# Fifteen gate units of two gated feed-forward layers computed with seven half-size products instead of eight, with part of the extra work on GpSimd

## The chip, the cores and the metric

The kernel runs on one NeuronCore of a Trainium2 chip. The metric is the time of one execution on the device in microseconds. The median of 3 runs before the change is 1631.95 us.

## The reference

Two transformer blocks act one after the other on 512 rows of width 1024, all in float32. The change touches only the gated feed-forward of the second block, which comes twice (l = 0 and 1; below "layer 0" and "layer 1"):

```python
def conv_ffn(h, w_gate, w_val, conv_w, conv_b, w_out):
    a = h @ w_gate                                   # 512x1024 @ 1024x2816
    ap = jnp.pad(a, ((0, 0), (CONV_W - 1, 0), (0, 0)))
    a = ap[:, 0:S] * conv_w[0] + ap[:, 1:S + 1] * conv_w[1] + ap[:, 2:S + 2] * conv_w[2] + conv_b
    return (jax.nn.silu(a) * (h @ w_val)) @ w_out
```

Ahead of it stands an RMS norm of h. The first block has an ungated MLP (4096 wide, squared ReLU), in which 11 of 16 "up" units are already computed in the way that the change brings to the gates.

## The kernel before

**Units.** All weights come from HBM as units of up to 128x2048 floats (1 MB), in a fixed list, PLAN. A unit of a gate or value matrix holds 256 output features for all 1024 inputs, so 11 gate units and 11 value units make a layer (`gate0 0` to `gate0 10`, `val0 0` and so on), and `fo0 0` to `fo0 11` are the units of the output matrix. Gate and value units alternate; the four output units of a group of pairs come after the first pair of the next group: gate 0, val 0, ..., gate 4, val 4, fo 0 to 3, gate 5, ..., val 8, fo 4 to 7, gate 9, ..., val 10, fo 8 to 11.

**Precision.** Each float32 operand is split into a high part (rounded to the type that TensorE takes) and a low part (what is left). ScalarE makes the high part of a unit (WH from RAW, line 1493), VectorE the low part (WL, line 1914); both together are called a split here. A product is then three matmuls: high by high, high by low, low by high (lines 728 to 730). The activations' parts are AH and AL, 8 tiles of 128x512. A normal unit is 2 output tiles of 8 x 3 matmuls with 512 columns, so 48 matmuls.

**Buffers.** RAW has two units, WH and WL have three, and each is used in turn. So a unit can be split while the two units before it are in TensorE. PSUM has 8 banks; FFN tiles take 7 of them in turn (`next_bank(7)`), and a bank is free again when VectorE has read it.

**Work behind a tile.** A gate tile m: VectorE multiplies PSUM by the norm's factors rb (line 2571) and does the three taps of the convolution (2573, 2575, 2577), ScalarE does SiLU (1833). A value tile m: VectorE multiplies by rb (2581) and by the gate (2583), ScalarE makes the high part HH (1838), VectorE the low part HL (2585), and ten such tiles (NH) are kept for the output units.

**Order.** Every engine walks the same generator (`ffn_order`) and does its own share of each step, waiting on counting semaphores. The order on an engine is thus the order in the code: in the turn of unit u first the split of unit u + 2, then the two tiles of u and what follows them. An engine never passes a waiting instruction. SyncE loads the units in order, each as soon as RAW is free.

**The fast form.** For the "up" units in FAST the weight unit is held as 2x2 blocks of 512 columns and the activations as 2x2 blocks of 256 rows (Winograd's form of Strassen's scheme). Seven products of half size, called a, c, g, d, e, b, f in the order in which TensorE does them, each of 4 x 3 matmuls with 256 columns, take the place of eight: 84 matmuls of 256 columns. It takes seven weight blocks (four raw or summed in place, three sums in `stage`; `added` makes the sums) and as many activation blocks (TH and TL, made by `shapes`), and the results are put together with extra additions (`mid`, `turned`, `row1`, `row2`). The seven blocks lie in a ring of 12 places, WHR and WLR, which is the same memory as WH and WL; a normal unit takes four.

Of the kernel before, what the change touches and what calls it, by code (L numbers as in the profile page):

```python
# [133 lines left out]
def low_is_in(k, m):  # L134

    return (k.POOL if UNIT["up", m // 2] in FAST else k.DVE)("hl", "down", m)

# [108 lines left out]
def memory(nc, ctx):  # L246
# [106 lines left out]
    a.at = inner  # L353
    k.cvs = [a.tile(f"cvs{i}", [P, S]) for i in range(2)]
# [88 lines left out]
def turn_order(u):  # L443
# [21 lines left out]
    if u + 1 in FAST:  # L465
        yield "part", u + 1, "stageA"
    if after and fast:
        yield "post", m
    if fast:
        yield "mid", u  # L470
        yield "turned", u
    if after and fast:
        yield "low", m
    if u + 1 in FAST:
        yield "part", u + 1, "stageB"
    if fast:
        yield "row2", u
        yield "post", 2 * i + 1
# [34 lines left out]

def ffn_order(l):

    pairs = ffn_pairs()
    for g in range(4):
        if g < 3:
            yield from pair_order(l, pairs[g][0])
        if g > 0:  # L520
            for i in range(4):
                yield "split", UNIT[f"fo{l}", 4 * (g - 1) + i] + 2
                yield "down", g - 1, 2 * i
                yield "down", g - 1, 2 * i + 1
        for j in pairs[g][1:] if g < 3 else ():
            yield from pair_order(l, j)
# [183 lines left out]
def tensor_program(k, e):  # L710
# [426 lines left out]
    def down(name, g, n, base, kc, m):  # L1137
# [36 lines left out]
    def form_product(u, x, bs):  # L1174
# [16 lines left out]
    def fast_products(u):  # L1191

        m = 2 * PLAN[u][1]
        bs = range(4) if PLAN[u][1] % 2 else range(4, 8)
# [3 lines left out]
        form_product(u, "a", bs)  # L1198
        w.wait_ge(WLO("stageB", u))
        form_product(u, "c", bs)  # L1200
        w.wait_ge(*free[bs[2]])
        form_product(u, "g", bs)
        form_product(u, "d", bs)
        w.wait_ge(*free[bs[3]])
        form_product(u, "e", bs)
        w.wait_ge(*free[bs[1]])
        form_product(u, "b", bs)
        form_product(u, "f", bs)
        for name in (("up", m), ("up", m + 1), ("unit", u)):
            MM.also(*name)  # L1210
        free[bs[0]], free[bs[1]], free[bs[2]], free[bs[3]] = [DVE("y", u)], [DVE("row", m)], [DVE("row", m + 1)], [DVE("z", u)]

    for step, *x in mlp_order():
# [31 lines left out]
        elif step == "mid":  # L1245
            fast_products(*x)
# [70 lines left out]
    def ffn(l, norm, n0, added):  # L1317
        for step, *x in ffn_order(l):
# [31 lines left out]
            elif step == "tile":  # L1350
                y, m = x
                u = UNIT[f"{('gate', 'val')[y]}{l}", m // 2]
                b = next_bank(7)
# [127 lines left out]
def scalar_program(k, e):  # L1481
    w = Waits(e)
    bank, cst, par, X, AH, sq, t2s = k.bank, k.cst, k.par, k.X, k.AH, k.sq, k.t2s
    MM, ACT, DVE, POOL, WHI = k.MM, k.ACT, k.DVE, k.POOL, k.WHI
# [217 lines left out]

    def free_high(name, m, n0, group_of):
# [19 lines left out]
    for step, *x in mlp_order():  # L1723
# [18 lines left out]
        elif step == "part":  # L1742
            u, part = x
            w.wait_ge(loaded(k, u), DVE("s2" if part[:5] == "stage" else "s4", u),
                      *(MM(*name) for name in held_until(u, *PARTS[part])))
            for h, _, cols in ring_views(k, u, *PARTS[part]):
                t = e.activation(h, part_source(k, u, part)[:, cols], AF.Copy)  # L1747
            t.then_inc(*WHI.mark(part, u))
        elif step == "mid":
            u, = x  # L1750
            before = max((v for v in FAST if v < u), default=0)
# [67 lines left out]

    def ffn(l, norm, n0, seen):  # L1820
        name = f"fo{l}"
        group_of = lambda m: min(m // 8, 2)
        for step, *x in ffn_order(l):
# [77 lines left out]
def vector_program(k, e):  # L1901
# [497 lines left out]

    def added(u):  # L2400

        raw = k.RAW[RAW_OF[u]][:, :].rearrange("p (c n) -> p c n", c=4)
        before = max((v for v in FAST if v < u), default=0)
# [29 lines left out]
    for step, *x in mlp_order():  # L2433
# [14 lines left out]
        elif step == "part":  # L2448
            u, part = x
            w.wait_ge(WHI(part, u))  # L2450
            for h, l, cols in ring_views(k, u, *PARTS[part]):
                t = e.tensor_tensor(l, part_source(k, u, part)[:, cols], h.bitcast(F), SUB)  # L2452
            t.then_inc(*WLO.mark(part, u))
            if part == "rawB":
                WLO.also(u)
# [95 lines left out]

    def ffn(l, norm, n0):
        name = f"fo{l}"
        for step, *x in ffn_order(l):
# [6 lines left out]
            elif step == "rest":  # L2561
                y, m = x
                i, s = m % 2, m % NH
                a, t, v = k.t1s[i], t2s[i], k.cvs[i]
                w.wait_ge(MM("ffn", l, y, m), ACT("rb", norm))
                if y == 0:
                    tap = [par[:, PC_CW + 66 * l + 22 * j + m:PC_CW + 66 * l + 22 * j + m + 1] for j in range(3)]
                    w.wait_ge(POOL("zeroed", l))
                    if m > 1:
                        w.wait_ge(DVE("conv", l, m - 2), DVE("gated", l, m - 2))  # L2570
                    e.tensor_tensor(a[:, 2:], bank[where["ffn", l, 0, m]][:, :], rb[:, :], MUL).then_inc(*DVE.mark("ffn", l, 0, m))
                    w.wait_ge(DVE("ffn", l, 0, m))
                    e.tensor_scalar(t[:, :], a[:, 0:S], tap[0], None, MUL).then_inc(*DVE.mark("tap0", l, m))
                    w.wait_ge(DVE("tap0", l, m))
                    e.scalar_tensor_tensor(t[:, :], a[:, 1:S + 1], tap[1], t[:, :], MUL, ADD).then_inc(*DVE.mark("tap1", l, m))
                    w.wait_ge(DVE("tap1", l, m))
                    e.scalar_tensor_tensor(t[:, :], a[:, 2:S + 2], tap[2], t[:, :], MUL, ADD).then_inc(*DVE.mark("conv", l, m))  # L2577
                else:
                    if m > 1:
                        w.wait_ge(DVE("hl", name, m - 2))  # L2580
                    e.tensor_tensor(v[:, :], bank[where["ffn", l, 1, m]][:, :], rb[:, :], MUL).then_inc(*DVE.mark("ffn", l, 1, m))
                    w.wait_ge(DVE("ffn", l, 1, m), ACT("silu", l, m))
                    e.tensor_tensor(v[:, :], v[:, :], t[:, :], MUL).then_inc(*DVE.mark("gated", l, m))  # L2583
                    w.wait_ge(ACT("hh", name, m))
                    e.tensor_tensor(k.HL[s][:, :], v[:, :], k.HH[s][:, :].bitcast(F), SUB).then_inc(*DVE.mark("hl", name, m))
# [89 lines left out]
def pool_program(k, e):  # L2675
# [17 lines left out]

    w.wait_ge((k.x_in[7], 16))
# [54 lines left out]
    root(4)  # L2749
# [19 lines left out]
    root(6)  # L2769
# [202 lines left out]
```

## Time and profile before

| | us |
|---|---|
| median of 3 runs (1630.81 to 1632.61) | 1631.95 |
| the profiled execution | 1633.97 |
| its span | 1632.2 |
| TensorE busy | 1625.4 |
| VectorE busy | 1015.7 |
| ScalarE busy | 660.1 |
| GpSimd busy | 115.0 |

The profile is of one execution. "Busy" of an engine is the time in which it had an instruction running; "span" is from the first to the last instruction. Layer 0 of the feed-forward runs from about 656 to 1018 us, layer 1 from about 1268 us to the end. Matmuls are pipelined, so the distance between two starts, not the duration of one, is what a matmul costs.

### The profile page before, as it was taken

How to read it: one execution, taken by the hardware profiler on the slowest of the kernel's cores; microseconds unless marked ns; L12 is line 12 of the kernel's file. 1: busy time of each engine (PE TensorE's matmuls, PEld its weight loads, DVE VectorE, ACT ScalarE, POOL GpSimd, SP SyncE). 2: the span in 40 equal slices, each digit the busy share in tenths (PEclk: the TensorE clock that was granted, in tenths of full speed). 3: DMA queues.
4: the chain of work that ended last, by engine and by line, in shares of the span. 5: the costliest groups of instructions: out<-in, count | busy, mean ns of one | idle time of the engine just before them, and what ended most of it. 6: DMA issues, size and time to landing. Idle time of an engine off the chain costs nothing.

```text
span 1632.2 us, 20194 instructions
## 1 busy us (share of the span) xinstructions
PE 1625.4 (100%) x8480; PEld 1347.1 (83%) x8480; DVE 1015.7 (62%) x1523; ACT 660.1 (40%) x919; POOL 115.0 (7%) x102
## 2 busy tenths in 40 slices
PE   9999999999999999999999999999999999999999
PEld 7877878898989888888888888877777888888887
DVE  6797664696756757577466357546655576366353
ACT  5576435344444446433222223456565333122221
POOL 1300000011111100000000000312101100000000
PEclk9999999999999999999999999999999999999999
DMA  5310228355464521223222213322221223222311
GB/s 188 112 41 27 104 78 120 82 111 138 86 138 85 162 78 64 80 102 116 104 103 90 111 64 123 102 87 94 76 77 52 78 103 108 100 102 97 110 59 71
DMA packets 28059, 156.01 MB, mean 96 GB/s; under 512 B 3712, under 2 KB 5392, under 8 KB 12096
## 3 DMA queue, kind: packets, MB, share of 16 engines
q1 hardware_dynamic: 26352, 149.75, 25.8%
q0 software_dynamic: 1328, 4.86, 5.3%
q8 instruction: 67, 1.10, 0.3%
q14 instruction: 24, 0.20, 0.0%
q10 hardware_dynamic: 288, 0.10, 0.0%
HBM read 149.98 MB, written 4.72 MB: 95 GB/s over the span
## 4 chain that ended last, share of the span: by engine, by line
PE 75%; DVE 2%; ACT 1%; issue 1%; POOL 0%; DVEq 0%; ACTq 0%
PE bank L728 20%; PE bank L729 19%; PE bank L730 19%; PE bank L734 3%; PE bank L736 2%; PE bank L735 2%; PE bank L1186 2%; PE bank L1188 2%; PE bank L1187 2%; PE bank L1424 1%; PE bank L1434 1%; PE bank L1450 1%; DVE WLR L2452 1%; PE bank L1310 0%; ACT WHR L1747 0%
## 5 line engine op out<-in xcount | busy, mean ns | idle before, releaser
L1914 DVE TENSOR_TENSOR WL<-RAW,WH 128x2048 fp32r<-128x2048 f32 (+2 forms) x122 | 273.0, 2243 | 193.5 <-ACT WH L1493 193.5
L728 PE MATMUL bank<-AH,WH 128*128 128x512 f32 (+1 forms) x974 | 382.9, 393 | 0.4 <-DVE WL L1964 0.3
L730 PE MATMUL bank<-AH,WL 128*128 128x512 f32 (+1 forms) x974 | 379.2, 389 | 0.0
L729 PE MATMUL bank<-AL,WH 128*128 128x512 f32 (+1 forms) x974 | 379.2, 389 | 0.0
L1493 ACT ACTIVATE WH<-RAW 128x2048 fp32r<-128x2048 f32 (+2 forms) x122 | 227.0, 1867 | 171.9 <-PE bank L730 138.0
L728 PE MATMUL bank<-HH,WH 128*128 128x512 f32 x608 | 236.6, 389 | 0.0
L729 PE MATMUL bank<-HL,WH 128*128 128x512 f32 x608 | 236.5, 389 | 0.0
L730 PE MATMUL bank<-HH,WL 128*128 128x512 f32 x608 | 236.5, 389 | 0.0
L728 PEld LDWEIGHTS bank<-AH,WH 128*128 128x128 f32 (+1 forms) x974 | 182.5, 187 | 41.9 <-issue 2.4
L730 PEld LDWEIGHTS bank<-AH,WL 128*128 128x128 f32 (+1 forms) x974 | 182.5, 187 | 38.8
L729 PEld LDWEIGHTS bank<-AL,WH 128*128 128x128 f32 (+1 forms) x974 | 182.5, 187 | 38.3 <-issue 1.0
L730 PEld LDWEIGHTS bank<-HH,WL 128*128 128x128 f32 x608 | 114.1, 188 | 23.8
L728 PEld LDWEIGHTS bank<-HH,WH 128*128 128x128 f32 x608 | 114.1, 188 | 23.7
L729 PEld LDWEIGHTS bank<-HL,WH 128*128 128x128 f32 x608 | 114.1, 188 | 23.4
L1944 DVE TENSOR_TENSOR X<-X,bank 128x512 f32<-128x512 f32 x79 | 54.0, 685 | 117.5 <-PE bank L730 117.5
L1833 ACT ACTIVATE t2s<-t2s,par 128x512 f32<-128x512 f32 x44 | 31.9, 724 | 186.6 <-DVE t2s L2577 186.6
L734 PE MATMUL bank<-WH,AH 128*128 128x512 f32 x224 | 89.9, 401 | 0.0
L736 PE MATMUL bank<-WH,AL 128*128 128x512 f32 x224 | 87.5, 391 | 0.0
L735 PE MATMUL bank<-WL,AH 128*128 128x512 f32 x224 | 87.3, 390 | 0.0
L1838 ACT ACTIVATE HH<-cvs 128x512 fp32r<-128x512 f32 x44 | 27.8, 633 | 126.0 <-DVE cvs L2583 126.0
L1500 ACT ACTIVATE sq<-X 128x512 f32<-128x512 f32 x49 | 30.9, 630 | 59.4 <-DVE X L1944 55.3
L734 PEld LDWEIGHTS bank<-WH,AH 128*128 128x128 f32 x224 | 42.0, 188 | 10.8 <-issue 2.3
(347 smaller groups left out, 2379.3 us busy)
## 6 DMA issues: line engine op xcount, KB each, us to landing
RAW<-in_W SPq DMA_DIRECT2D x124, 1024.0 KB, 4.8
RAW<-in_W SPq DMA_DIRECT2D x9, 768.0 KB, 4.2
X<-in_XT SPq DMA_DIRECT2D x16, 256.0 KB, 5.5
ev_scratch<-ev POOLq DMA_DIRECT2D x16, 160.0 KB, 7.6
Gb<-ev_scratch SPq DMA_DIRECT2D x16, 128.0 KB, 3.1
Gb<-ev_scratch SPq DMA_DIRECT2D x16, 112.0 KB, 2.7
out<-X SPq DMA_DIRECT2D x7, 256.0 KB, 2.0
RAW<-in_W SPq DMA_DIRECT2D x2, 512.0 KB, 6.0
```

Source lines behind the costliest of these rows:

```text
L728: e.matmul(o, a, h, start=first, stop=False)
L729: e.matmul(o, a, l, start=False, stop=False)
L730: return e.matmul(o, c, h, start=False, stop=last)
L734: e.matmul(o, h, a, start=first, stop=False)
L735: e.matmul(o, h, c, start=False, stop=False)
L736: return e.matmul(o, l, a, start=False, stop=last)
L1186: e.matmul(o, a, h, start=c == 0 and x in "ageb", stop=False, skip_group_check=True)
L1187: e.matmul(o, a, lo, start=False, stop=False, skip_group_check=True)
L1188: t = e.matmul(o, l, h, start=False, stop=c == 3, skip_group_check=True)
L1493: e.activation(k.WH[SLOT_OF[u]][:, 0:n], k.RAW[RAW_OF[u]][:, 0:n], AF.Copy).then_inc(*WHI.mark(u))
L1914: e.tensor_tensor(k.WL[j][:, 0:n], k.RAW[RAW_OF[u]][:, 0:n], k.WH[j][:, 0:n].bitcast(F), SUB).then_inc(*WLO.mark(u))
L1944: e.tensor_tensor(X[:, m, :], X[:, m, :], src, ADD).then_inc(*DVE.mark("x", n, m))
```

## The change

Fifteen gate units join FAST: `gate0 4` to `gate0 10` and `gate1 3` to `gate1 10`. The order of the units stays. What comes with it:

- the activations' blocks FH and FL (four forms of 256 columns for each of 4 chunks c), made once a layer, in the turns of three early units (FORMS_IN): GpSimd adds high and low parts ("sum", two instructions of 128x512), VectorE makes four forms ("form", four of 128x256), ScalarE makes their high parts (two of 128x512), GpSimd their low parts ("formed", two of 128x512);
- the weight sums of a fast gate are made on GpSimd (one instruction of 128x1024 and two of 128x512, step "add"), in the turn of the unit two before it; its seven blocks are split in four parts ("part": 1024, 1024, 1024 and 512 columns) on ScalarE and VectorE in the turn of the unit just before it;
- the low parts HL of value tiles go from VectorE to GpSimd;
- the first tap of the fast tiles goes to ScalarE;
- the value tile's own buffer (cvs) is gone: the gate's tile t2s is multiplied by rb and then by the value's PSUM tile, so a value tile's bank is free only after that second multiplication (`DVE.also("ffn", l, 1, m)`);
- steps "mid", "turned", "row1", "row2" and "conv" put a fast gate's tiles together.

```diff
+FIRST_GATE = (4, 3)
 FAST = {UNIT["up", i] for i in range(FIRST_FAST, 16)}
+FAST |= {UNIT[f"gate{l}", j] for l in range(2) for j in range(FIRST_GATE[l], 11)}
...
+FORMS_IN = ({("gate", 2): (0, 1), ("val", 2): (2,), ("gate", 3): (3,)},
+            {("gate", 1): (0, 1), ("val", 1): (2,), ("gate", 2): (3,)})
 def ffn_order(l):
+    first = 2 if l == 0 else 1
+    for j in range(first):
+        yield from pair_order(l, j)
+    for u in range(UNIT[f"gate{l}", first], UNIT[f"fo{l}", 11] + 1):
+        yield from ffn_turn(l, u)
+def ffn_turn(l, u):
+    for c in forms:
+        yield "sum", c
+    if behind:
+        yield "row1", u - 1
+    if u + 1 in FAST:
+        for part in PARTS:
+            yield "part", u + 1, part
+    for v in (u + 1, u + 2):
+        if v < len(PLAN) and v not in FAST and turn_of(v) == u:
+            yield "split", v
+    for c in forms:
+        yield "form", c
+        yield "formed", c
+    if u + 2 in FAST:
+        yield "add", u + 2
+    if fast:
+        yield "mid", u
+        yield "turned", u
+        yield "row2", u
+    elif name == "fo":
+        yield "down", i // 4, 2 * (i % 4)
+        yield "down", i // 4, 2 * (i % 4) + 1
+    else:
+        if behind:
+            yield "conv", i
+        for m in (2 * i, 2 * i + 1):
+            yield "tile", int(name == "val"), m
+            yield "rest", int(name == "val"), m
...
+    def set_of(u):
+        return range(4) if PLAN[u][1] % 2 else range(4, 8)
+    def fast_gate(l, u):
+        w.wait_ge(*(POOL("formed", l, c) for c in range(4)))
+        bs = fast_products(u, k.FH, k.FL, "dceg")
...
+            elif step == "form":
+                w.wait_ge(POOL("sum", l, c))
+                if c > 0:
+                    w.wait_ge(POOL("formed", l, c - 1))
...
+            elif step == "sum":
+                if c > 0:
+                    w.wait_ge(DVE("f4", l, c - 1))
+                for i, z in enumerate((k.stage[:, 2, :], k.fx[c][:, :])):
+                    t = e.tensor_tensor(z, k.AH[:, 4 * i + c, :].bitcast(F), k.AL[:, 4 * i + c, :].bitcast(F), ADD)
+                t.then_inc(*POOL.mark("sum", l, c))
+            elif step == "formed":
+                for n in range(2):
+                    w.wait_ge(ACT("fh", l, c, n), DVE("f4", l, c))
+                    t = e.tensor_tensor(k.FL[:, c, 2 * n:2 * n + 2, :], k.stage[:, n, :].rearrange("p (i n) -> p i n", i=2),
+                                        k.FH[:, c, 2 * n:2 * n + 2, :].bitcast(F), SUB)
+                t.then_inc(*POOL.mark("formed", l, c))
```

How the change moves instructions at three places. First, VectorE in layer 0 before the change, from the end of gate unit 2 to the beginning of value unit 3 (WL is a unit's low part, cvs and HL belong to a value tile, t1s and t2s to a gate tile):

```order
L1914 TENSOR_TENSOR WL_59<-RAW_54,WH_56 128x2048
L2581 TENSOR_TENSOR cvs_169<-bank,rb 128x512
L2583 TENSOR_TENSOR cvs_169<-cvs_169,t2s_69 128x512
L2585 TENSOR_TENSOR HL_140<-cvs_169,HH_130 128x512
...
L1914 TENSOR_TENSOR WL_60<-RAW_55,WH_57 128x2048
L2571 TENSOR_TENSOR t1s_146<-bank,rb 128x512
...
L1914 TENSOR_TENSOR WL_61<-RAW_54,WH_58 128x2048
L2581 TENSOR_TENSOR cvs_169<-bank,rb 128x512
```

The same place after the change (WLR is the ring of low parts; the four WLR instructions are the parts of `gate0 4`, the first fast gate):

```order
L2676 TENSOR_TENSOR t1s_147<-bank,rb 128x512
L2678 TENSOR_SCALAR t2s_70<-t1s_147,par 128x512
L2656 SCALAR_TENSOR_TENSOR t2s_70<-t1s_147,par,t2s_70 128x512
L2658 SCALAR_TENSOR_TENSOR t2s_70<-t1s_147,par,t2s_70 128x512
L2497 TENSOR_TENSOR WLR<-RAW_55,WHR 128x1024 x2
L2497 TENSOR_TENSOR WLR<-stage,WHR 128x1024
L2497 TENSOR_TENSOR WLR<-stage,WHR 128x512
L2682 TENSOR_TENSOR t2s_69<-t2s_69,rb 128x512
L2684 TENSOR_TENSOR t2s_69<-t2s_69,bank 128x512
```

Before, the weights of gate unit 4 were split ahead of the two tiles of gate unit 3; now its parts stand behind them, one unit before TensorE wants them, and only the two value tiles of unit 3 follow.

Second, GpSimd in layer 0 after the change, from the low parts of value tiles 2 and 3 to the sums of the first fast gate. Before, GpSimd had nothing here at all.

```order
L2848 TENSOR_TENSOR HL3_139<-t2s1_70,HH3_129 128x512
L2857 TENSOR_TENSOR stage_65<-AH_52,AL_53 128x512
L2857 TENSOR_TENSOR fx0_171<-AH_52,AL_53 128x512
...
L2863 TENSOR_TENSOR FL_170<-stage_65,FH_169 128x512 x4
...
L2848 TENSOR_TENSOR HL5_141<-t2s1_70,HH5_131 128x512
L2857 TENSOR_TENSOR stage_65<-AH_52,AL_53 128x512
L2857 TENSOR_TENSOR fx3_174<-AH_52,AL_53 128x512
L2863 TENSOR_TENSOR FL_170<-stage_65,FH_169 128x512 x2
L2871 TENSOR_TENSOR stage_65<-RAW1_55 128x1024
L2874 TENSOR_TENSOR stage_65<-RAW1_55,stage_65 128x512
L2876 TENSOR_TENSOR RAW1_55<-RAW1_55,stage_65 128x512
```

All sums, forms' low parts, value tiles' low parts and weight sums stand in one queue.

Third, VectorE in layer 1 after the change, around the parts of `gate1 3`, the first fast gate there (with the bank numbers):

```order
L2497 TENSOR_TENSOR WLR_63<-RAW1_55,WHR_62 128x1024 x2
L2497 TENSOR_TENSOR WLR_63<-stage_65,WHR_62 128x1024
L2497 TENSOR_TENSOR WLR_63<-stage_65,WHR_62 128x512
L2682 TENSOR_TENSOR t2s0_69<-t2s0_69,rb_64 128x512
L2684 TENSOR_TENSOR t2s0_69<-t2s0_69,bank6 128x512
L2682 TENSOR_TENSOR t2s1_70<-t2s1_70,rb_64 128x512
L2684 TENSOR_TENSOR t2s1_70<-t2s1_70,bank0 128x512
```

and TensorE's first matmul of that unit:

```order
L1226 MATMUL bank0<-AH_52,WHR_62 128x256
```

The last of the four instructions on value tiles reads bank 0, into which the first product of the fast gate writes.

## Rows read from the trace of the kernel before

**Rows 1.** The page's first part: busy time of each engine.

```profile
PE 1625.4 (100%) x8480; PEld 1347.1 (83%) x8480; DVE 1015.7 (62%) x1523; ACT 660.1 (40%) x919; POOL 115.0 (7%) x102
```

**Rows 2.** TensorE's waits: for whom, us in total, times, longest.

```profile
PE bank L1186 <- DVE WLR L2452: 0.8, 2, 0.4
```

**Rows 3.** TensorE's timeline, at three borders between units of the feed-forwards.

```profile
810.81 0.39 PE L728 MATMUL bank<-AH,WH 128*128 128x512 f32 x1
...
897.85 0.39 PE L728 MATMUL bank<-HH,WH 128*128 128x512 f32 x1
...
1378.76 0.39 PE L728 MATMUL bank<-HH,WH 128*128 128x512 f32 x1
```

**Rows 4.** TensorE's timeline, four fast up units: starts of products a, g, d, e.

```profile
423.86 0.28 PE L1186 MATMUL bank<-AH,WHR 128*128 128x256 f32 x1
...
426.67 0.28 PE L1186 MATMUL bank<-AH,WHR 128*128 128x256 f32 x1
...
428.09 0.29 PE L1186 MATMUL bank<-TH,WHR 128*128 128x256 f32 x1
...
429.47 0.28 PE L1186 MATMUL bank<-TH,WHR 128*128 128x256 f32 x1
...
463.21 0.40 PE L728 MATMUL bank<-HH,WH 128*128 128x512 f32 x1
```

**Rows 5.** VectorE's timeline, layer 0, in brackets the idle time before and its releaser.

```profile
698.10 0.68 DVE L2581 TENSOR_TENSOR cvs<-bank,rb 128x512 f32<-128x512 f32 x1
...
704.74 2.29 DVE L1914 TENSOR_TENSOR WL<-RAW,WH 128x2048 fp32r<-128x2048 f32 x1 [1.11 <-ACT WH L1493]
...
721.18 0.69 DVE L2571 TENSOR_TENSOR t1s<-bank,rb 128x512 f32<-128x512 f32 x1
...
723.88 0.69 DVE L2571 TENSOR_TENSOR t1s<-bank,rb 128x512 f32<-128x512 f32 x1
...
729.26 2.29 DVE L1914 TENSOR_TENSOR WL<-RAW,WH 128x2048 fp32r<-128x2048 f32 x1 [2.60 <-ACT WH L1493]
731.47 0.68 DVE L2581 TENSOR_TENSOR cvs<-bank,rb 128x512 f32<-128x512 f32 x1
732.19 0.69 DVE L2583 TENSOR_TENSOR cvs<-cvs,t2s 128x512 f32<-128x512 f32 x1
...
745.05 0.75 DVE L2577 SCALAR_TENSOR_TENSOR t2s<-t1s,par,t2s 128x512 f32<-128x512 f32 x1
```

**Rows 6.** ScalarE's timeline, layer 0: SiLU of gate tile 5 and the split behind it.

```profile
726.70 0.72 ACT L1833 ACTIVATE t2s<-t2s,par 128x512 f32<-128x512 f32 x1 [1.97 <-DVE t2s L2577]
727.33 1.90 ACT L1493 ACTIVATE WH<-RAW 128x2048 fp32r<-128x2048 f32 x1
```

**Rows 7.** GpSimd's timeline in the MLP: low parts of up tiles.

```profile
364.29 1.67 POOL L2734 TENSOR_TENSOR HL<-t2s,HH 128x512 fp32r<-128x512 f32 x1 [3.24 <-ACT HH L1721]
...
384.73 1.30 POOL L2734 TENSOR_TENSOR HL<-t2s,HH 128x512 fp32r<-128x512 f32 x1 [0.56 <-ACT HH L1721]
```

**Rows 8.** Groups by shape in the MLP (330 to 545 us): busy us, mean ns.

```profile
L2452 DVE TENSOR_TENSOR WLR<-RAW,WHR 128x1024 fp32r<-128x1024 f32 x20 | 23.7, 1222 | 6.7 <-ACT WHR L1747 6.7
...
L2459 DVE TENSOR_TENSOR YZ<-G,bank 128x256 f32<-128x256 f32 x11 | 4.6, 418 | 2.6 <-ACT G L1753 2.6
...
L1747 ACT ACTIVATE WHR<-RAW 128x1024 fp32r<-128x1024 f32 x20 | 20.2, 1053 | 51.2 <-DVE RAW L2410 34.1 <-PE bank L730 9.4 <-issue 7.7
```

**Rows 9.** VectorE's timeline, layer 1: the first gate tile.

```profile
1293.29 0.69 DVE L2571 TENSOR_TENSOR t1s<-bank,rb 128x512 f32<-128x512 f32 x1
```

**Rows 10.** TensorE in one stretch: busy us (instructions), granted clock, DMA share, GB/s.

```profile
192.00:198.40 6.40, 6.40 (x18) 0.50 0.00 0
```

**Rows 11.** TensorE's timeline ahead of and in the stretch of rows 10.

```profile
190.58 2.33 PE L1075 MATMUL bank<-cst,sq 128*128 128x1 f32 x16
...
194.20 0.63 PE L728 MATMUL bank<-OM,WH 128*128 128x512 f32 x1
194.63 0.63 PE L729 MATMUL bank<-LM,WH 128*128 128x512 f32 x1
```

More of the change, by code:

```diff
@@ L352, in memory @@
               enumerate([base + 4 * S * 8] + [base + 4 * S * (NH + 8) + 4 * 4 * BW * i for i in range(3)])]
-    a.at = inner
-    k.cvs = [a.tile(f"cvs{i}", [P, S]) for i in range(2)]
+    a.at = inner + 192
+    k.FH = a.tile("FH", [P, 4, 4, 256], R)
+    fl_at = a.at
+    k.FL = a.tile("FL", [P, 4, 4, 256], R)
+    k.fx = [a.over(f"fx{c}", [P, S], fl_at + 4 * 1024 * c) for c in range(4)]
     a.at = base
@@ L466, in turn_order @@
         yield "part", u + 1, "stageA"
+        yield "part", u + 1, "stageB"
     if after and fast:
         yield "post", m
+        yield "low", m
     if fast:
@@ L471, in turn_order @@
         yield "turned", u
[L472 to L476, printed above, removed]
         yield "row2", u
@@ L511, in up_order @@
             yield "rest", m
+FORMS_IN = ({("gate", 2): (0, 1), ("val", 2): (2,), ("gate", 3): (3,)},
+            {("gate", 1): (0, 1), ("val", 1): (2,), ("gate", 2): (3,)})
 def ffn_order(l):
[L516 to L526, printed above, removed]
+    first = 2 if l == 0 else 1
[4 more added lines that the diff above has]
+def ffn_turn(l, u):
+    name, i = PLAN[u][0][:-1], PLAN[u][1]
+    fast, behind = u in FAST, u - 1 in FAST
+    forms = FORMS_IN[l].get((name, i), ())
+    for c in forms:
[26 more added lines that the diff above has]
+            yield "rest", int(name == "val"), m
 def pair_order(l, j):
@@ L1699, in scalar_program, with part_high @@
     split(UNIT["up", 0] + 1)
+    def part_high(u, part, adder):
+        w.wait_ge(loaded(k, u))
+        if part != "rawA":
+            w.wait_ge(adder("s2" if part[:5] == "stage" else "s4", u))
+        w.wait_ge(*(MM(*name) for name in held_until(u, *PARTS[part])))
+        for h, _, cols in ring_views(k, u, *PARTS[part]):
+            t = e.activation(h, part_source(k, u, part)[:, cols], AF.Copy)
+        t.then_inc(*WHI.mark(part, u))
     def free_high(name, m, n0, group_of):
@@ L1743, in scalar_program @@
             u, part = x
[L1744 to L1748, printed above, removed]
+            part_high(u, part, DVE)
         elif step == "mid":
             u, = x
-            before = max((v for v in FAST if v < u), default=0)
+            before = fast_before(u)
             w.wait_ge(MM("form", u, "c"), DVE("row", 2 * PLAN[before][1]) if before else DVE("t4", 3))
@@ L2448, in vector_program @@
         elif step == "part":
[L2449 to L2455, printed above, removed]
+            part_low(*x)
         elif step == "mid":
@@ L2768, in pool_program @@
     t.then_inc(*POOL.mark("zeroed", 1))
-    root(6)
+    ffn(1, 6)
 def sync_program(k, e):
```

209 lines of the change are left out of this document (160 added, 49 removed).

## The prediction

> **What bounds the kernel now.** I read the page's busy shares first: TensorE is busy 1625.4 of 1632.2 us, VectorE 62% [rows 1]. Then TensorE's waits: the longest kind in the whole program is 0.8 us in two waits, on the weights of fast up units, and none falls into the feed-forwards [rows 2]. So the time is TensorE's issue time, and a change gains what it takes from that and loses every wait that it makes. Third, TensorE's timeline: eight units from 810.81 to 897.85 take 87.04 us, 10.88 each, with nothing between [rows 3].
>
> The lower shares of the others do not mean that they keep up. Value tile 0 of layer 0 was begun by VectorE at 698.10, and gate unit 3's last tap ends at 745.8 [rows 5]. Counting back six units from 810.81, gate unit 4 starts in TensorE at 745.53, value unit 3 at 734.65 [rows 3]. VectorE thus stands a unit behind TensorE after each norm. Today that costs nothing, since weights are split two units ahead.
>
> **What the change removes.** Four fast up units take 39.35 us, 9.84 each; a product that reads AH takes 1.42 (426.67 to 428.09), one that reads TH 1.38 [rows 4]. In the new gates product g reads the made forms too, and most of the others follow a made one, so I take 9.77. A unit saves 1.11 us, fifteen 16.6. Bounds: 9.84 gives 15.6; FH no faster than AH, at some 0.12 per matmul (84 x 0.12 = 10.08), gives 12.0.
>
> **What it adds, steady state.** Per pair VectorE gains 1536 split columns and the five combinations, and loses two HL and two first taps. Worked from one gate's start: split of the value unit done at +6.4, combinations by +8.3, first row at +10.6 behind product f, the four parts by +15, taps by +20.3, last value tile by +22.3, that is 1.6 us into the next gate, as it began. TensorE wants the value weights at +9.8 and the next gate's at +20.6, so it has 3.4 and more to spare: 0 us. GpSimd has some 8 us per 20.6. If that cover went, each pair would lose what is missing. Only at the last value unit is the new route of HL (high part on ScalarE, 0.63 to the next as between 726.70 and 727.33, then GpSimd 1.3) [rows 6, 7] a little late for the sixth chunk of `fo 8`: 0.3 us a layer.
>
> **What it adds at the start of each layer.** This decides. The row prices: gate tile 2.70 (721.18 to 723.88), two-instruction value tile 1.42 (pitch 0.72 and 0.70), a split in VectorE 2.21, a split that begins behind the last tap's SiLU 2.66 later (726.6 to 729.26) [rows 5, 6]; GpSimd 1.30 per 512 columns with two inputs, where 1.67 occurs [rows 7]; a part of 1024 columns 1.05 on ScalarE and 1.22 on VectorE, 256 columns 0.42 [rows 8], so four forms 1.7 (estimate). For 1024 columns on GpSimd I take 2 x 1.30.
>
> Layer 0 from 698.10, in program order. VectorE: value tiles 0 and 1 to 700.9; split of val 2 (behind ScalarE's) 703.4 to 705.65; gate tiles 2 and 3 to 711.05; value tiles to 713.9; split of gate 3 to 718.6. GpSimd's low parts end at 715.9, its first sum at 718.5. Form 0 to 720.3. Now form 1 needs sum 1 and "formed 0", four GpSimd instructions behind form 0: 725.5; form 1 to 727.3. Gate tiles 4 and 5 to 732.7. The split of val 3 is queued behind their SiLU: 735.3 to 737.5, and TensorE wants it at 734.65: **2.9 us**. Form 2 to 739.2, value tiles to 742.05. Form 3 needs sum 3, which stands behind formed 2 and two low parts, six instructions: 747.1; form 3 to 748.8. Gate tiles 6 and 7 to 754.2. Only now the parts of gate 4: ScalarE's first 754.9, VectorE's 756.0 to 757.2. TensorE ended val 3 at 748.4: **8.8 us**. GpSimd's weight sums (formed 3, then 5.2) end at 756.7, so rawB is done at 759.0 and stageB, for which product c waits, at 760.9. Product a ends at 758.6: **2.3 us**. Layer 0: 14.0.
>
> Layer 1 from 1293.29 [rows 9], one unit earlier in everything; gate 3 would start at 1378.76 - 4 x 10.88 = 1335.2 [rows 3]. The same walk: split of val 2 at 1325.15 against 1324.36, **0.8**; form 1 waits to 1313.2, form 3 to 1334.8; gate tiles to 1341.9; rawA at 1344.85, stageB at 1348.55. Here the first product also writes bank 0, which held value tile 5, and that bank is free only after its second multiplication, four instructions (2.8) behind the parts: 1351.4. TensorE is free at 1336.1: **15.3 us**, and c waits no more. Layer 1: 16.1. Without the bank it would be 8.8 + 2.3 as above, 4.2 less.
>
> Behind this VectorE is level with TensorE, and the later fast gates start without a wait.
>
> **TensorE's clock.** From 192.0 to 198.4 us the granted clock is 0.50, the lower level of 1.2 GHz, and 512-column matmuls stand 0.43 apart, not 0.227; just before, the engine did 16 matmuls of one column in 2.33 us [rows 10, 11]. An idle of 9 or 15 us should lower it too. Lost there: 6.4 x (1 - 0.227/0.43) = 3.0 us. Part of it falls into the wait for c in layer 0, so I take 1.5 + 3.0 = **4.5 us**, bounds 0 and 6.
>
> The Trainium skill, "TensorE: Matmul & The Clock Gate", section "HAM oscillation — how this bites in real kernels", says that gaps in which TensorE idles throttle it again and the work behind them runs at the lower clock. Its idle case is not in this trace; by the row alone, which has only light work, the 4.5 might be 0, and the sum 1646.
>
> **Sum.** -16.6 + 14.0 + 16.1 + 0.6 + 4.5 = +18.6. The profiled execution, 1633.97, becomes 1652.6; the median of the runs, 1631.95, lies 2 us below and becomes 1650.6, 1.1% slower. GpSimd at 1.67 instead of 1.30 on the ten instructions that form 1 and form 3 wait for costs 3.7 a layer, +7.4; FH at AH's pace +4.6; no clock loss -4.5; no bank wait -4.2.
>
> **Rivals.**
> *Faster: the start costs less than the gain.* Place: the first fast gates; mechanism: VectorE is not held by GpSimd, so sums and low parts run ahead. With the two waits per layer (5.2 and 5.0) and the bank wait gone, VectorE reaches the parts some 10 us earlier, about 744, and each layer loses 3 to 4: -16.6 + 7 = 1622. It decides in favour when a layer's start costs under 8.3 us. For it: GpSimd is idle here today [rows 1]. Against: each form waits for instructions that cannot be issued earlier, and the order is fixed. Chance 0.11.
> *GpSimd is slower than its rows.* The 128x1024 sums with a broadcast operand, and all sums beside VectorE, cost 1.67 per 512 or more. Starts +7.4, and if a low part then comes too late in each pair, 1 us on each of 15: 1660 to 1672. For it: rows of 1.67 while VectorE works; against: most rows are 1.30, and VectorE mostly waits there. Chance 0.17.
> The skill, "GPSIMD Engine Reference", section "Elementwise — side-by-side cycle accounting", holds that a two-input operation takes GpSimd about twice VectorE's time because both inputs share one read port. By that rule this work should stay where it was; 1.30 against 0.69 agrees.
> *The early stalls are there but TensorE gains nothing else*, the half-size products at 0.12: inside the range. *The change does nothing to the time* (gain and starts cancel at 8.3 a layer): 0.04.
>
> **How the numbers follow.** Forecast 0.68, slower by GpSimd 0.17, faster 0.11, same 0.04. Three runs tell 0.2% from nothing. The range leaves out the faster case and most of the second: low, no clock loss, no bank wait and 3 us of luck in waits, 1639; high, half of GpSimd's surcharge and FH's pace, 1660.
>
> **What would show it.** Right: a new wait of TensorE on VectorE's WLR of about 9 us near 748 and one of about 15 near 1336 on a value tile's second multiplication; two VectorE waits on GpSimd of about 5 us ahead of each; granted clock 0.5 behind both; units at 9.8 with no wait from the second fast gate on. Wrong: the parts of the first fast gate done before TensorE is free; or waits in every pair, on WL (VectorE too late) or on the sums (GpSimd too slow).

## The result and the profile after

The changed kernel takes 1664.27 us (median of 4 runs, 1664.17 to 1665.38) against 1632.28 of before (4 runs, 1630.81 to 1633.17): ratio 1.0201, 95% interval 1.0188 to 1.0213. It is 32 us slower where 18.6 were forecast: the sign is right, the time lies above the range. The profiled execution has a span of 1662.5 us, 30.3 more than before.

The page's first part; columns as in [rows 1]:

```profile
PE 1615.6 (97%) x9020; PEld 1363.0 (82%) x9020; DVE 1076.5 (65%) x1601; ACT 720.3 (43%) x1025; POOL 313.0 (19%) x223
```

TensorE now does less (1615.6 us busy, 1625.4 before) and is no longer always busy. GpSimd's busy time has gone from 115.0 to 313.0. The second view is the list of TensorE's waits (for whom, us in total, times, longest), which answers to [rows 2]:

```profile
PE bank L1226 <- DVE t2s L2684: 16.5, 1, 16.5
PE bank L768 <- DVE WL L2007: 12.8, 2, 7.3
PE bank L1226 <- DVE WLR L2497: 12.3, 1, 12.3
```

These four waits are 41.6 us, all ahead of or at the first fast gate of a layer, and no later unit waits. TensorE's timeline gives their places: value unit 3 and gate unit 4 of layer 0, value unit 2 and gate unit 3 of layer 1, with the matmul that follows each of the two gates, and one later fast gate for comparison:

```profile
737.63 0.79 PE L768 MATMUL bank<-AH,WH 128*128 128x512 f32 x1 [7.28 <-DVE WL L2007]
...
762.48 0.55 PE L1226 MATMUL bank<-AH,WHR 128*128 128x256 f32 x1 [12.26 <-DVE WLR L2497]
...
774.92 0.40 PE L768 MATMUL bank<-AH,WH 128*128 128x512 f32 x1
...
829.35 0.28 PE L1226 MATMUL bank<-AH,WHR 128*128 128x256 f32 x1
...
839.10 0.40 PE L768 MATMUL bank<-AH,WH 128*128 128x512 f32 x1
...
850.01 0.28 PE L1226 MATMUL bank<-AH,WHR 128*128 128x256 f32 x1
...
1342.27 0.80 PE L768 MATMUL bank<-AH,WH 128*128 128x512 f32 x1 [5.50 <-DVE WL L2007]
...
1372.69 0.55 PE L1226 MATMUL bank<-AH,WHR 128*128 128x256 f32 x1 [16.46 <-DVE t2s L2684]
...
1383.83 0.40 PE L768 MATMUL bank<-AH,WH 128*128 128x512 f32 x1
```

A later fast gate takes 839.10 - 829.35 = 9.75 us, and with the value unit behind it, to 850.01, 20.66 where the pair took 2 x 10.88 before: 1.10 less, so the gain is as forecast (1.11). The first ones take 12.44 (762.48 to 774.92) and 11.14 (1372.69 to 1383.83). The value units ahead of them take 12.59 (737.63 to 750.22, where the next wait begins) and 13.96 (1342.27 to 1356.23) instead of 10.88. The granted clock behind each wait says why (TensorE in a stretch, as in [rows 10], with the other engines between):

```profile
737.70:740.70 3.00, 3.00 (x7) 2.41 (x8) 2.86 (x7) 1.38 (x3) 1.38 (x1) 0.50 0.74 216
741.00:750.00 9.00, 9.00 (x41) 7.32 (x39) 3.42 (x8) 1.89 (x4) 7.13 (x6) 1.00 0.08 32
762.50:768.00 5.50, 5.50 (x25) 5.43 (x26) 5.18 (x7) 1.59 (x4) 0.76 (x1) 0.50 0.57 194
768.00:775.00 7.00, 7.00 (x62) 7.00 (x62) 4.07 (x5) 2.63 (x3) 1.82 (x2) 1.00 0.15 39
1342.30:1348.00 5.70, 5.70 (x14) 4.44 (x15) 4.24 (x8) 2.41 (x4) 4.04 (x3) 0.50 0.50 184
1372.70:1375.60 2.90, 2.90 (x13) 2.90 (x14) 0.56 (x1) 2.31 (x2) 2.77 (x3) 0.50 0.02 6
```

The first, third, fifth and sixth stretch, one behind each of the four waits, are at 0.50, the lower level of 1.2 GHz; together the four units behind waits are 2.7 + 1.4 + 1.7 + 3.1 = 8.9 us too long.

So the span splits into -16.6 (gain), +41.6 (waits), +8.9 (clock), and -4.5, because VectorE's first gate tile of layer 0 comes that much earlier than before (688.24 against 692.70). Some 2.9 of this is the half-clock stretch of [rows 10], which this execution does not have. The rest are the first four fast up units, which take 39.35 where they took 40.91; 0.8 of that are the two waits of [rows 2], and the change, which also reorders some steps of the fast up units, has neither. The sum is +29.4 of the 30.3.

Now VectorE's timeline in layer 0, gate tile 6 and the start of tile 7, the last work ahead of the first fast gate's parts; in the prediction such a tile costs 2.70:

```profile
749.02 0.69 DVE L2676 TENSOR_TENSOR t1s<-bank,rb 128x512 f32<-128x512 f32 x1
749.75 1.23 DVE L2678 TENSOR_SCALAR t2s<-t1s,par 128x512 f32<-128x512 f32 x1
751.01 1.65 DVE L2656 SCALAR_TENSOR_TENSOR t2s<-t1s,par,t2s 128x512 f32<-128x512 f32 x1
752.69 2.71 DVE L2658 SCALAR_TENSOR_TENSOR t2s<-t1s,par,t2s 128x512 f32<-128x512 f32 x1
755.33 0.68 DVE L2676 TENSOR_TENSOR t1s<-bank,rb 128x512 f32<-128x512 f32 x1
```

And GpSimd's in the same layer, first behind the low parts of value tiles 2 and 3, then beside the rows above:

```profile
712.60 3.37 POOL L2857 TENSOR_TENSOR fx<-AH,AL 128x512 f32<-128x512 f32 x1
717.64 1.29 POOL L2857 TENSOR_TENSOR stage<-AH,AL 128x512 f32<-128x512 f32 x1 [1.67 <-DVE stage L2699]
...
752.25 2.60 POOL L2871 TENSOR_TENSOR stage<-RAW 128x1024 f32<-128x1024 f32 x1
```

The tap that begins at 752.69 takes 2.71, and the GpSimd sum that is under way ends at 754.85. GpSimd's own sum at 712.60 takes 3.37: VectorE's split was running then (711.86, for 2.94) and ended at 714.80. The one at 717.64, beside an idle VectorE, takes 1.29. Rows that read a bank keep their 0.68. Summed over VectorE's operations from 688 to 762 us, 8.6 us are above their durations in the kernel before, and 8.9 in the same part of layer 1 (1305 to 1373 us); VectorE's waits for GpSimd, 5.27 and 5.41, are as forecast (5.2 and 5.0). That is the theory to be tested: **contention**, VectorE's operations whose tensors are all in SBUF stretched by GpSimd's. The rival is **waits only**: VectorE's standing for GpSimd costs the time, and the long rows have another cause.

### The profile page after: what moved, and what is told of

It is laid out like the page before. It is cut to its first block, busy times and chain, and to the rows that moved or that the text cites. A ratio compares the mean times of both kernels' runs of the same rounds, so it can differ in the third digit from the quotient of the medians.

```text
span 1662.5 us, 21669 instructions
## 1 busy us (share of the span) xinstructions
PE 1615.6 (97%) x9020; PEld 1363.0 (82%) x9020; DVE 1076.5 (65%) x1601; ACT 720.3 (43%) x1025; POOL 313.0 (19%) x223
## 4 chain that ended last, share of the span: by engine, by line
PE 88%; DVE 6%; POOL 3%; ACT 2%; issue 1%; DMA 0%; SPq 0%; DVEq 0%
PE bank L768 18%; PE bank L769 18%; PE bank L770 18%; PE bank L1226 5%; PE bank L1228 5%; PE bank L1227 5%; PE bank L774 3%; PE bank L776 3%; PE bank L775 3%; PE bank L1484 1%; PE bank L1023 1%; PE bank L1494 1%; PE bank L1510 1%; DVE t2s L2656 1%; DVE t2s L2658 1%; PE bank L1008 1%
## 5 line engine op out<-in xcount | busy, mean ns | idle before, releaser
L768 PE MATMUL bank<-AH,WH 128*128 128x512 f32 (+1 forms) x734 | 291.8, 398 | 13.2 <-DVE WL L2007 12.8
L769 PE MATMUL bank<-AL,WH 128*128 128x512 f32 (+1 forms) x734 | 287.6, 392 | 0.0
L770 PE MATMUL bank<-AH,WL 128*128 128x512 f32 (+1 forms) x734 | 287.3, 391 | 0.0
L768 PEld LDWEIGHTS bank<-AH,WH 128*128 128x128 f32 (+1 forms) x734 | 138.5, 189 | 45.7 <-DVE WL L2007 13.6
L770 PEld LDWEIGHTS bank<-AH,WL 128*128 128x128 f32 (+1 forms) x734 | 138.4, 189 | 29.9
L1226 PE MATMUL bank<-AH,WHR 128*128 128x256 f32 x356 | 101.7, 286 | 28.7 <-DVE t2s L2684 16.5
L2848 POOL TENSOR_TENSOR HL<-t2s,HH 128x512 fp32r<-128x512 f32 x44 | 56.9, 1294 | 318.1 <-ACT HH L1908 316.2
L1770 ACT ACTIVATE WHR<-RAW 128x1024 fp32r<-128x1024 f32 (+1 forms) x54 | 53.8, 1022 | 138.8 <-PE bank L770 75.9
L1228 PE MATMUL bank<-AH,WLR 128*128 128x256 f32 x356 | 101.6, 285 | 0.0
L1227 PE MATMUL bank<-AL,WHR 128*128 128x256 f32 x356 | 101.4, 285 | 0.0
L1226 PEld LDWEIGHTS bank<-AH,WHR 128*128 128x128 f32 x356 | 68.8, 193 | 30.1 <-issue 29.5
```

The lines of the kernel that those rows point to most:

```text
L768: e.matmul(o, a, h, start=first, stop=False)
L769: e.matmul(o, a, l, start=False, stop=False)
L770: return e.matmul(o, c, h, start=False, stop=last)
L1226: e.matmul(o, a, h, start=c == 0 and x in "ageb", stop=False, skip_group_check=True)
L1227: e.matmul(o, a, lo, start=False, stop=False, skip_group_check=True)
L1228: t = e.matmul(o, l, h, start=False, stop=c == 3, skip_group_check=True)
```

## The experiments

Each line tells the edit against the changed kernel, unless it says otherwise. Beside the runs stands the kernel before on the same chip: 1631.78 (runs 1 to 4), 1632.26 (5 to 8) and 1631.81 (9).

**1. No fast gates, no forms.**

```
FIRST_GATE = (11, 11)
FORMS_IN = ({}, {})
```

> Control: the changed kernel with no fast gate and no form; what is left of the change are the low parts of value tiles on GpSimd, values in the gate's tile and the banks. In the trace of the changed kernel the excess over before is 41.6 us of waits at the first fast gates, some 9 us of clock behind them, 16.6 us of gain, and a start of layer 0 that is 4.4 us earlier. If that account is right, without gates and forms the time is that of before, 1632, within 2 us (low parts of the sixth chunk late by 0.3 a layer, clock period at 192 us there or not). If instead GpSimd's low parts slow VectorE in every pair so much that TensorE waits, it is 1636 or more.

One wait that named the last part of a fast gate names the plain unit's weights here.

Measured: 1629.18 us (10 runs), ratio 0.9989 (0.9979 to 0.9998); no wait of TensorE in the feed-forwards. Values in the gate's tile, their low parts on GpSimd and the banks cost nothing. That it is 2.6 us less than before fits the two differences ahead of layer 0 named above: no half-clock stretch in the profiled execution, and 39.35 us for the first four fast up units. The 0.6 us for the sixth chunk of `fo 8` is not there. All that is lost comes with the forms and the fast gates.

**2. Forms in the fo turns, first fast gate at gate 5.**

```
FIRST_GATE = (5, 5)
FORMS_IN = ({("fo", 0): (0, 1), ("fo", 1): (2,), ("fo", 2): (3,)},) * 2
```

> Forms in the turns of fo 0 to 2 and the first fast gate at gate 5 in both layers: 12 fast gates instead of 15. All theories that put the loss at the start of a layer, where VectorE stands a unit behind, say that the waits go: gain 12 x 1.11 = 13.3, start costs 0, 0.6 for the sixth chunk: 1632.3 - 13.3 + 0.6 = 1619.6, within 2; no wait of TensorE above 1 us. If the contention of GpSimd and VectorE also costs where VectorE has slack, the forms in the fo turns bring waits of some us a layer and the time is 1624 to 1630. If the fast gates do not gain what the borders of units say, it is 1630 or more.

Measured: 1618.26 us (4 runs), ratio 0.9920 (0.9905 to 0.9935): faster than both kernels. TensorE waits for nothing here, while VectorE still waits for GpSimd as long as ever (for whom, total, times, longest):

```profile
DVE stage L2693 <- POOL fx L2856: 15.7, 6, 4.2
DVE stage L2693 <- POOL FL L2862: 10.5, 2, 5.3
```

These 26.2 us cost nothing: they lie where VectorE has only to add blocks to X. Against run 1 twelve gates bring 10.9 us by the medians and 12.0 between the fastest executions (1628.62 and 1616.57); by the borders of units it would be 12 x 1.10 = 13.2. Between the profiled executions it is 10.5, and some 1.7 more when the half-clock stretch, which only run 2's has (granted clock 0.83 from 190 to 200 us), is set aside; about 1 us stays unexplained.

**3. Forms and the first weight sums on VectorE, in their old places.**

```
-    for c in forms:
+    for c in forms[:1]:
         yield "sum", c
...
     for c in forms:
         yield "form", c
+        if c + 1 in forms:
+            yield "sum", c + 1
         yield "formed", c
```

The steps "sum", "formed" and the first fast gate's "add" are taken from GpSimd's program into VectorE's, with the same operations.

> The forms' sums and low parts and the first fast gate's weight sums on VectorE instead of GpSimd; nothing else is moved. Work added on VectorE ahead of the first fast gate: 8 sums of 0.69, 8 low parts of 0.75, weight sums 2.6, in all 14.1 us; waits of VectorE for GpSimd that go: 1.2 + 5.3 + 5.4 = 11.9 us. Contention theory (VectorE's operations with all inputs in SBUF are stretched while GpSimd runs its two-input operations, 8.6 us in the trace of layer 0): the stretch goes too, the first product of gate0 4 stands 6 to 9 us earlier than in the changed kernel (754 to 756 instead of 762.5) and the same in layer 1: 1664.3 - 13 to 18 = 1646 to 1651; the taps of gate tiles 4 to 7 take 0.49, 0.75, 0.75. Waits-only theory (what cost is VectorE standing for GpSimd, the long taps are something else, as traffic of DMA or of ScalarE): 14.1 - 11.9 = 2.2 us later a layer, long taps stay: 1668.

Measured: 1650.96 us (4 runs), ratio 1.0122 (1.0105 to 1.0139), 13.3 less than the changed kernel. The same gate tile 6 in VectorE's timeline:

```profile
746.48 0.68 DVE L2678 TENSOR_TENSOR t1s<-bank,rb 128x512 f32<-128x512 f32 x1
747.19 0.48 DVE L2680 TENSOR_SCALAR t2s<-t1s,par 128x512 f32<-128x512 f32 x1
747.71 0.75 DVE L2658 SCALAR_TENSOR_TENSOR t2s<-t1s,par,t2s 128x512 f32<-128x512 f32 x1
748.50 0.75 DVE L2660 SCALAR_TENSOR_TENSOR t2s<-t1s,par,t2s 128x512 f32<-128x512 f32 x1
```

and the first product of gate unit 4 in TensorE's:

```profile
755.05 0.55 PE L1228 MATMUL bank<-AH,WHR 128*128 128x256 f32 x1 [11.83 <-DVE WLR L2499]
```

It begins 7.4 us earlier than in the changed kernel (762.48), although VectorE has 13.6 us more work even at undisturbed durations (16 instructions of 0.69 and 2.6 of weight sums), and every tap has its old duration. Waits only had this kernel 2.2 us a layer later; it falls. What stays is VectorE's lateness itself: TensorE still waits 11.8 and, in layer 1, 17.4 us.

**4. Value tile 5 of layer 1 in bank 4.**

```
b = ... if u - 1 in FAST else 4 if (l, y, m) == (1, 1, 5) else next_bank(7)
```

> Only the bank of value tile 5 of layer 1 is changed, from 0 to 4, so that the first product of gate1 3 does not wait for that tile's second multiplication. In the trace of the changed kernel the part that product a needs is ready at 1366.9 (first half of the pair of low parts from 1365.66), product a began at 1372.69; with stageB ready at 1369.75 product c then waits under 1 us. Expected: 5 us less, 1659.3, in the place of TensorE's 16.5 us wait one of some 11 us on the weights. The prediction had 4.2 for this step. If the bank is not what ends the wait, the time stays 1664.

Measured: 1660.99 us (4 runs), ratio 1.0181 (1.0165 to 1.0196): 3.3 less, not 5.0 (4.5 less between the profiled executions, whose layers 1 begin at the same time, 1305.54 and 1305.56). TensorE's timeline in layer 1:

```profile
1354.33 0.80 PE L768 MATMUL bank<-AH,WH 128*128 128x512 f32 x1 [4.09 <-DVE t1s L2676]
...
1367.06 0.55 PE L1226 MATMUL bank<-AH,WHR 128*128 128x256 f32 x1 [5.66 <-DVE WLR L2497]
```

The first product begins where its weights are done, at 1367.06, 5.6 earlier: the bank was what ended the wait. But bank 4 held a gate tile that the late VectorE had not read, so the value tile waited 4.1, and the gate behind the shorter waits took 11.85, 0.7 more than 11.14. My expectation had looked at one wait and not at the next.

**5. GpSimd at side work in the kernel before.** Sixteen sums of two tiles that nothing else touches, then sixteen copies; nobody waits for them.

```
+    for n in range(32):
...
+        if n < 16:
+            t = e.tensor_tensor(k.side[n % 2][:, :], k.side[2][:, :], k.side[3][:, :], ADD)
+        else:
+            t = e.tensor_copy(k.side[n % 2][:, :], k.side[2][:, :])
```

> The kernel before, with work for GpSimd that nobody reads or waits for, in the first gate tiles of layer 0: 16 sums of two tiles of 128x512, then 16 copies of one such tile. VectorE's program is unchanged, and none of its tiles is touched by GpSimd. Contention theory: beside the sums VectorE's first tap goes from 0.49 to about 1.2, the other taps from 0.75 to about 1.65, a split from 2.29 to about 2.9, while multiplications that read a bank stay at 0.69; sums take more than 1.30 there. Beside the copies the stretch is smaller or none, if it is a matter of GpSimd's second input; if it is the same, any work of GpSimd does it. Theory of other traffic: VectorE's rows stay as before. The time stays within 2 us of before, since VectorE's work has cover of about a unit.

VectorE beside the sums, from 690 to 716 us, by shape (busy us, mean ns):

```profile
L2576 DVE SCALAR_TENSOR_TENSOR t2s<-t1s,par,t2s 128x512 f32<-128x512 f32 x3 | 5.0, 1664 | 0.1
...
L2574 DVE TENSOR_SCALAR t2s<-t1s,par 128x512 f32<-128x512 f32 x3 | 3.2, 1072 | 0.1
L2572 DVE TENSOR_TENSOR t1s<-bank,rb 128x512 f32<-128x512 f32 x4 | 2.7, 680 | 0.0
L2584 DVE TENSOR_TENSOR cvs<-cvs,t2s 128x512 f32<-128x512 f32 x2 | 2.1, 1062 | 0.1
```

the same operations with GpSimd idle, from 726 to 767 us:

```profile
L2576 DVE SCALAR_TENSOR_TENSOR t2s<-t1s,par,t2s 128x512 f32<-128x512 f32 x4 | 3.0, 751 | 0.1
L2584 DVE TENSOR_TENSOR cvs<-cvs,t2s 128x512 f32<-128x512 f32 x4 | 2.8, 693 | 0.1
...
L2574 DVE TENSOR_SCALAR t2s<-t1s,par 128x512 f32<-128x512 f32 x4 | 1.9, 486 | 0.1
```

the first gate tile beside the copies, in VectorE's timeline:

```profile
767.30 0.92 DVE L2574 TENSOR_SCALAR t2s<-t1s,par 128x512 f32<-128x512 f32 x1
768.25 0.98 DVE L2576 SCALAR_TENSOR_TENSOR t2s<-t1s,par,t2s 128x512 f32<-128x512 f32 x1
```

and GpSimd's two kinds, from 690 to 800 us:

```profile
L2762 POOL TENSOR_TENSOR side<-side,side 128x512 f32<-128x512 f32 x16 | 27.3, 1743 | 11.9 <-DVE t1s L2572 11.9
L2764 POOL COPY side<-side 128x512 f32<-128x512 f32 x16 | 13.8, 909 | 49.1 <-DVE t1s L2572 49.1
```

A tap goes from 0.75 to 1.66, the first tap (one tensor input, in SBUF, 0.49) to 1.07 in the mean (0.79 to 1.62), a product of two SBUF tiles from 0.69 to 1.06; what reads a bank stays at 0.68. The one split that lies wholly beside the sums takes 2.50 where it took 2.29; 2.9 was expected. Beside copies a tap takes 0.98. In the kernel before, with GpSimd idle, the gate tile at 692.70 has its first tap at 0.48 and the others at 0.75, so it is not the place in the layer. The contention is shown, without any dependence between the engines. The rest of my expectation was wrong: the time was 1641.54 (one execution), 9 more, as VectorE was slowed so much that TensorE waited 6.4 us for gate unit 3's weights. The unit of cover that I had counted was not there so soon behind the norm.

**6. TensorE held ahead of five gates of the kernel before**, for chains of 1, 2, 4, 6 and 9 sums of GpSimd.

```
LADDER = {5: 1, 6: 2, 7: 4, 9: 6, 10: 9}
...
+    w.wait_ge(POOL("held", m // 2, LADDER[m // 2] - 1))
```

> The kernel before, in which TensorE stands still ahead of gate units 5, 6, 7, 9 and 10 of layer 0, for a chain of 1, 2, 4, 6 and 9 sums of GpSimd: about 1.3, 2.6, 5.4, 8 and 12 us. It measures the clock term alone. In the changed kernel idle times of 5.5, 7.3, 12.3 and 16.5 us were followed by granted clock 0.5 and by units that were about 3.0, 1.6, 2.7 and 1.4 us too long. If any idle time of some us costs about the same, the units behind the last three are 1.5 to 3 us too long whatever its length, and those behind 1.3 and 2.6 us show whether there is a length that costs nothing. If the price grows with the idle time, 12 us cost twice what 5.4 do. Whole time: 1632 + 29 idle + 6 to 9 clock = 1667 to 1670, and less where VectorE's lead is given back nowhere.

Measured: 1669.91 us (one execution), span 1668.1. The idle times, in TensorE's timeline:

```profile
809.01 0.50 PE L730 MATMUL bank<-AH,WH 128*128 128x512 f32 x1 [1.18 <-POOL side L2760]
833.73 0.79 PE L730 MATMUL bank<-AH,WH 128*128 128x512 f32 x1 [2.62 <-POOL side L2760]
862.36 0.80 PE L730 MATMUL bank<-AH,WH 128*128 128x512 f32 x1 [5.18 <-POOL side L2760]
960.74 0.79 PE L730 MATMUL bank<-AH,WH 128*128 128x512 f32 x1 [8.69 <-POOL side L2760]
997.61 0.80 PE L730 MATMUL bank<-AH,WH 128*128 128x512 f32 x1 [12.16 <-POOL side L2760]
```

and the clock in the stretch behind each:

```profile
809.00:816.00 7.00, 6.99 (x31) 5.75 (x32) 3.43 (x3) 0.85 (x1) 0.00 (x0) 1.00 0.35 137
833.70:844.00 10.30, 10.27 (x39) 8.40 (x40) 5.50 (x6) 1.82 (x2) 0.00 (x0) 0.86 0.29 103
862.30:873.00 10.70, 10.64 (x36) 8.63 (x37) 4.55 (x5) 0.00 (x0) 0.00 (x1) 0.76 0.28 98
960.70:971.00 10.30, 10.26 (x33) 8.20 (x34) 1.76 (x3) 0.00 (x0) 0.00 (x0) 0.72 0.00 0
997.60:1008.00 10.40, 10.39 (x40) 8.48 (x41) 2.69 (x4) 0.42 (x1) 0.00 (x0) 0.86 0.00 0
```

The wait of 1.18 us was followed by no loss of clock. Behind the others (1 - clock) x length gives 1.4, 2.6, 2.9 and 1.5 us: 12.2 us of idle time cost no more than 2.6. The span grew by 35.9, of which 29.8 are idle time; the rest, 6.1, with the 3.0 of [rows 10] that this execution lacks, is near the sum 8.4. So each of the four longer waits cost one to three us of clock, and the changed kernel has four waits of such length.

**7. Fast gates in layer 0 alone.**

```
FIRST_GATE = (4, 11)
FORMS_IN = ({("gate", 2): (0, 1), ("val", 2): (2,), ("gate", 3): (3,)}, {})
```

> Fast gates and forms in layer 0 alone, as in the changed kernel; layer 1 as in the run without fast gates (1629.2). From the trace of the changed kernel layer 0 costs 19.6 us of waits and 4.3 of clock and gains 7 x 1.11 = 7.8: 1629.2 + 16.1 = 1645.3; layer 1 then costs the rest, 19. If the layers do not add (for instance because the clock or a late start of layer 1 depends on layer 0), it is off by more than 2.

Measured: 1645.70 us (4 runs), ratio 1.0081 (1.0066 to 1.0096). That is 16.5 over run 1 for layer 0, where its account gave 16.1, and leaves 18.6 for layer 1, where waits (22.0), clock (4.5) and the gain of eight gates (8.9) give 17.6. The layers add within 1 us.

**8. As run 2, with the forms' sums, low parts and the first weight sums on VectorE**, that is the edits of runs 2 and 3 together.

> Forms in the fo turns and first fast gate at gate 5 as in the run of 1618.3, but with the forms' sums and low parts and the first weight sums on VectorE. Contention and waits-only theory agree that VectorE has cover there (it stood for GpSimd 26 us in these turns without TensorE waiting): 1618.3 within 1.5. If the 11.5 us more on VectorE per layer eat that cover, 1620 to 1625; then GpSimd is of use there.

Measured: 1617.92 us (4 runs), ratio 0.9910 (0.9894 to 0.9927). The same as run 2 within what can be told. In the fo turns GpSimd does not help with the forms and its contention does not hurt.

**9. Forms in their old places, first fast gate at gate 5**, `FIRST_GATE = (5, 5)` alone.

> The two halves of the move that gave 1618.3 taken apart: the first fast gate is gate 5 in both layers, as there, but the forms stay where the changed kernel makes them, in the first turns behind the norm. By the timeline of the changed kernel the value weights of the last pair ahead of the forms' end are as late as there (7.3 us at val0 3, 5.5 at val1 2, and some 4.6 of clock behind them), while the weights of the plain gate that follows are split ahead of the last form and are not waited for, and the value weights behind it come with 0 to 1 us of wait: 1618.3 + 12.8 + 4.6 + 1 = 1636.7. If the forms' place costs nothing and only the parts of the first fast gate were late, the time is 1618 to 1620; if the whole loss comes with the forms, some 1650.

Measured: 1642.66 us (4 runs), ratio 1.0066 (1.0049 to 1.0083), 6 above my number. TensorE's waits:

```profile
PE bank L768 <- DVE WL L2007: 16.3, 4, 7.3
PE bank L768 <- DVE t2s L2684: 2.6, 1, 2.6
```

The 7.3 and 5.3 are as expected; but the next value units waited 1.8 each (I had 0 to 1), and the first block of `fo 0` 2.6 for a bank, at a granted clock of 0.85 behind it (783.8 to 794 us). So the forms' early place costs 24.4 us by itself (against run 2), and moving the first fast gate up to gates 4 and 3 adds 21.6 to that, although it brings three gates, 3.3 us.

## Why the prediction was wrong

**The gain** (16.6) is right: 9.75 a gate, 9.77 forecast, and 15 x 1.10 = 16.5 by pairs. A gate whose products read FH is no slower than a fast up unit (9.84), so that bound was not needed.

**The steady state** (0 us) is right: no wait behind the first fast gates, and run 1 shows it for GpSimd's low parts.

**The starts** are the failed step. The four waits were forecast as 2.9, 8.8, 0.8 and 15.3, with 2.3 for product c, 30.1 in all, and came as 7.28, 12.26, 5.50 and 16.46, with none for c: 41.5. The mechanism and all four places are right, and so are VectorE's waits for GpSimd. What failed are the prices in the walk: "gate tile 2.70", "a split in VectorE 2.21", and "GpSimd 1.30" for the first sum, each read where the other engine was idle or reading banks. With GpSimd at work, gate tile 6 of layer 0 takes 6.3 us (749.02 to 755.33), and the walk is 9 to 10 us short at the first fast gate of each layer: in layer 0, 8.6 of stretched rows and a wait of 1.2 for the first sum, which met VectorE's split. Runs 3 and 5 show that this is contention. The 2.3 for product c did not come, since its last part was done at 765.10 while product a, at the lower clock, ran until 765.18.

The Trainium skill, "SBUF — State Buffer", section "Who interferes with whom", calls the contention an exclusive lock on a pair of ports: a VectorE instruction with two SBUF inputs contends with a GpSimd instruction that reads SBUF, and so does one in a mode that uses both ports, where the first to issue holds them for its whole instruction; one with at most one SBUF input outside those modes does not contend. The rows agree with who is touched: 0.68 for bank rows, 2.71 for the tap that met a sum of 2.6, 3.37 for the sum that met a split. The first tap, with one SBUF input, is stretched too (0.49 to 1.07), which by that section it would be only in such a mode; that it ran in one is not shown here. And in run 5 the price is less than two full durations on end: a tap beside a sum takes 1.66, where 0.75 + 1.30 would be 2.05, and the measurement decides.

The sign that was there to be read: in [rows 7] the low part of 1.67 began while VectorE added `RAW<-RAW,stage`, both inputs in SBUF, and the one of 1.30 beside an idle VectorE. I took 1.67 as a spread of GpSimd's duration, priced it in a rival and by half in the upper bound, and did not ask what VectorE pays when GpSimd comes first. That rival, GpSimd slower than its rows, gives 1660 to 1672 and so holds the time, but by luck: VectorE's two waits for GpSimd per layer stayed as forecast, the 128x1024 sum took 2.60, and no pair in the steady state was late.

**The bank of value tile 5**: a step of 4.2 in the prediction, 3.3 by run 4 (4.5 between the profiled executions).

**TensorE's clock** is a term that was mis-sized: 4.5 forecast, 8.9 measured. I counted two drops, of 3.0 and 1.5. Each of the longer waits of run 6 (2.6 us and more) was followed by one, and here there were four, since the value units waited too. The bound of 6 was too low.

**The 0.6 us at `fo 8`** were not there, and the 4.5 us by which layer 0 came earlier were not in the sum.

In figures of the profiled executions: waits +11.5 against the forecast, clock +4.4, `fo 8` -0.6, the early start -4.5, which makes 10.8 of the 11.7 us by which the change of the span (30.3) passed the forecast (18.6).

## What to carry to other kernels

Work moved from VectorE to GpSimd is not off VectorE's path where VectorE's instructions beside it take all their tensors from SBUF: price both engines' instructions as stretched, above all where VectorE is already the late one (here 8.6 us in 74). Ask next where the late engine has slack: the same forms made some turns later, where VectorE only adds to X, with twelve fast gates instead of fifteen, turned +32 us into -14, and on either engine alike. When a change makes an always busy TensorE wait, count the clock too: here each wait of 2.6 us and more cost its length and one to three us of clock.

## What the runs showed of the hardware

- VectorE beside a stream of two-input GpSimd sums (run 5): three-operand tap 0.75 to 1.66 us, single-input scaling in SBUF 0.49 to 1.07 in the mean, two-input product 0.69 to 1.06, the product that reads a bank unchanged at 0.68. GpSimd's sums go from 1.30 to 1.74 themselves. Beside one-input copies the tap takes 0.98.
- Idle time of TensorE and its clock (runs 6 and 9 and the changed kernel): waits of 1.18 and 1.83 us left the granted clock at 1.00, those of 2.60 to 16.46 us were each followed by 0.50, and in run 6 and the changed kernel the loss of 1.4 to 3.1 us did not grow with the length.
- The half-clock stretch of [rows 10] comes in some executions and not in others: from 190 to 200 us the granted clock was 0.66 in the profiled execution of before and 0.83 in those of runs 2, 4, 8 and 9, but 1.00 in those of the changed kernel and of runs 1, 3 and 5 to 7. In run 1, executions at a mean clock of 0.999 have spans of 1629.0 and 1629.1, most of those at 1.000 have 1627.3.
